# A fused decoder layer whose expert stage packs its tokens into buffers of 96 rows instead of 128, with 18 weight chunks in flight

## What is computed

```python
def hier_moe(x, w_rg, b_rg, w_re, b_re, w_g, w_u, w_d):
    # top-1 of 4 groups, then the top 2 of the 4 experts inside it
    ...
    for e in range(N_EXPERTS):                      # 16
        h = jax.nn.silu(xt @ w_g[e]) * (xt @ w_u[e])   # 1024 -> 512
        out = out + gates[:, e:e + 1] * (h @ w_d[e])   # 512 -> 1024
```

## Time and profile before

| | |
|---|---|
| median of 3 runs | 971.64 us |
| lowest of 3 runs | 970.34 us |
| profiled execution | 972.64 us |
| span of its trace | 970.7 us |
| granted TensorE clock, mean | 0.964 of full |
| busy: PE, DVE, ACT | 907.7 (94%), 669.6 (69%), 491.5 (51%) us |
| weight splits, DVE L1726 | 96 of 2286 ns |
| loads of expert weights | 96 of 1 MB |

### The profile page before, as it was taken

One profiled execution on the slowest core, in us unless ns is written; L12 is line 12 of the kernel. 1 busy time (PEld: TensorE's weight loads), 2 busy tenths in 40 slices (PEclk: granted clock), 3 DMA queues, 4 the chain that ended last, 5 costly groups with the idle time before them and its releaser, 6 DMA issues.

```text
span 970.7 us, 14670 instructions
## 1 busy us (share of the span) xinstructions
PE 907.7 (94%) x5924; PEld 518.1 (53%) x5924; DVE 669.6 (69%) x877; ACT 491.5 (51%) x681; POOL 71.3 (7%) x89
## 2 busy tenths in 40 slices
PE   6999999999999998999999979928999999999884
PEld 4434784855766655444444449924455554545442
DVE  5677769541887775643344344557899999999887
ACT  5444373223454444233232324463787888888643
POOL 7000000003000000000000000010111211111000
PEclk9989999999999999999999989957999999999998
DMA  8702404527621102943443316255899999999742
GB/s 211 176 25 59 116 24 111 151 66 198 176 79 33 38 23 65 391 111 94 120 118 83 104 46 234 95 201 170 295 388 403 380 405 391 389 399 379 309 185 89
DMA packets 119454, 177.92 MB, mean 183 GB/s; under 512 B 14317, under 2 KB 99621, under 8 KB 107094
## 3 DMA queue, kind: packets, MB, share of 16 engines
q1 hardware_dynamic: 112176, 162.76, 48.8%
q0 software_dynamic: 6928, 13.61, 4.8%
q10 hardware_dynamic: 278, 0.56, 0.2%
HBM read 172.76 MB, written 16.22 MB: 195 GB/s over the span
## 4 chain that ended last, share of the span: by engine, by line
PE 88%; DVE 6%; ACT 3%; DMA 1%; issue 1%; DVEq 0%; ACTq 0%; POOLq 0%
PE bank L963 25%; PE bank L964 24%; PE bank L965 24%; PE bank L1176 3%; PE bank L1195 3%; PE bank L1306 2%; DVE arena L1726 1%; PE bank L1070 1%; PE bank L1185 1%; PE bank L1055 1%; ACT arena L839 1%; PE bank L1267 1%; PE bank L1314 1%; PE bank L1134 1%; DMA cst<-in_c_sq 1%
## 5 line engine op out<-in xcount | busy, mean ns | idle before, releaser
L963 PE MATMUL bank<-arena 128*128 128x512 f16 (+1 forms) x1568 | 466.6, 318 | 16.4 <-DVE arena L1832 6.0
L964 PE MATMUL bank<-arena 128*128 128x512 f16 (+1 forms) x1568 | 466.3, 318 | 0.0
L965 PE MATMUL bank<-arena 128*128 128x512 f16 (+1 forms) x1568 | 465.4, 317 | 0.0
L1726 DVE SCALAR_TENSOR_TENSOR arena<-arena 128x2048 f16<-128x2048 f32 x96 | 217.1, 2286 | 42.6 <-ACT arena L839 42.6
L963 PEld LDWEIGHTS bank<-arena 128*128 128x128 f16 x1568 | 155.7, 99 | 146.2 <-issue 36.5
L965 PEld LDWEIGHTS bank<-arena 128*128 128x128 f16 x1568 | 155.1, 99 | 112.6 <-issue 5.4
L964 PEld LDWEIGHTS bank<-arena 128*128 128x128 f16 x1568 | 154.9, 99 | 101.0 <-issue 4.9
L839 ACT ACTIVATE arena<-arena 128x2048 f16<-128x2048 f32 x96 | 181.5, 1908 | 24.8 <-PE bank L965 24.8
L606 ACT ACTIVATE arena<-arena 128x1024 f16<-128x1024 f32 (+1 forms) x92 | 92.5, 1007 | 101.9 <-PE bank L965 76.3
L1471 DVE SCALAR_TENSOR_TENSOR arena<-arena 128x1024 f16<-128x1024 f32 (+1 forms) x91 | 103.5, 1163 | 11.4 <-ACT arena L606 9.9
L660 ACT ACTIVATE arena<-bank 128x512 f32<-128x512 f32 x35 | 20.8, 595 | 92.3 <-PE bank L965 92.2
(11 more groups left out here) (275 smaller groups left out, 766.9 us busy)
## 6 DMA issues: line engine op xcount, KB each, us to landing
arena<-in_moe_wg SPq DMA_DIRECT2D x32, 1024.0 KB, 10.3
arena<-in_moe_wu SPq DMA_DIRECT2D x32, 1024.0 KB, 10.8
arena<-in_moe_wd SPq DMA_DIRECT2D x32, 1024.0 KB, 12.1
arena<-in_w_gate SPq DMA_DIRECT2D x32, 512.0 KB, 4.0
arena<-in_w_in SPq DMA_DIRECT2D x31, 512.0 KB, 3.9
arena<-in_w_branch SPq DMA_DIRECT2D x32, 192.0 KB, 3.6
y_rows<-in_c_tab SPq DMA_DIRECT2D x4, 1024.0 KB, 12.3
arena<-in_w_out SPq DMA_DIRECT2D x8, 512.0 KB, 5.0
```

What stands on the lines that cost most here:

```text
L963: pe.matmul(outb, lhs[0], rhs[0], start=first, stop=False, skip_group_check=True)
L964: pe.matmul(outb, lhs[0], rhs[1], start=False, stop=False, skip_group_check=True)
L965: return pe.matmul(outb, lhs[1], rhs[0], start=False, stop=last_, skip_group_check=True)
L1726: tell("split_done", stt(w_lo[c % NW], stage[c % NS], WSCALE, w_hi[c % NW], ALU.mult, ALU.subtract))
```

## The change

It touches the expert stage and the places of its buffers.

- CAP is 96: packed buffers, one-hots, gathers, scatters and transposes have 96 slots.
- Gate and up are turned round: the stationary operand is a 128 x 128 block of the weights, taken as every second column of a 256-column piece; the moving operand is the 96 packed tokens. A chunk has 48 matmuls of 96 columns instead of 12 of 512. The result has the hidden units on the partitions (`hid`, 4 x 96 = 384 columns), so that the four h transposes go away. Down keeps 12 matmuls of 512 columns per chunk, now with 96 tokens as stationary columns.
- The operations between them work on 384 columns instead of 512; `xg`, `xgT`, `sgr` and `hid` have one buffer instead of two.
- 12 staging buffers instead of 8 (`SLOT` maps chunks to them), 6 split pairs instead of 7 (18 chunks instead of 15), LOOK = 4 instead of 6. 15 loads are issued before the routing branch instead of 13, and the 16th needs no split.
- The scatter of expert e follows the gather of expert e+3 in POOL's queue instead of that of e+4. The four `add_rows` are done at the last four steps. The final norm's gains are loaded later.

```diff
-CAP = P
+CAP = 96
-LOOK = 6
+LOOK = 4
...
-        STAGE = [17408, 24576, 29696, 44172, 46220, 26624, 33292, 35340]
-        EARLY = 5
-        SPLIT = [40076, 42124, 37388, 0, 2048, 6144, 4096]
+        STAGE = [17408, 24576, 29696, 44172, 46220, 26624, 33292, 35340, 4096, 6144, 10752, 15360]
+        SPLIT = [(40076, 41100), (42124, 43148), (37388, 38412), (0, 1024), (2048, 3072), (28672, 31744)]
+        EARLY, READY = 5, 10
+        SLOT = [*range(READY), *range(FIRST), READY, FIRST, READY + 1]
+        for _c in range(len(SLOT), len(STEPS)):
+            SLOT.append(SLOT[_c - NS])
+        def splits_ahead(c):
+            return max((i + 1 for i in range(c) if SLOT[i] == SLOT[c]), default=0)
...
-                src = d["moe_w" + kind][0, e][k * P * hf:k * P * (hf + 1), :].rearrange("(p k) n -> p (k n)", k=k)
-                sp_.dma_start(stage[c % NS], src).then_inc(S(f"stage_landed{c % NS}"), 16)
+                src = d["moe_w" + kind][0, e][k * P * hf:k * P * (hf + 1), :]
+                src = src.rearrange("(p k) n -> p k n", k=k)
+                sp_.dma_start(stage[c].rearrange("p (k n) -> p k n", k=k), src).then_inc(S(f"stage_landed{SLOT[c]}"), 16)
...
-            for c in range(NS, NS + FIRST):
-                sp_.wait_ge(S("split_done"), c - NS + 1)
+            for c in range(READY, READY + FIRST):
+                sp_.wait_ge(S("split_done"), splits_ahead(c))
                 stage_load(c)
+                if c == READY + FIRST - 2:
+                    sp_.wait_ge(S("out_full"), KD)
+                    for j in (READY - 2, READY - 1):
+                        stage_load(j)
...
-                for c in range(NS + FIRST, len(STEPS)):
-                    sp_.wait_ge(S("split_done"), c - NS + 1)
+                for c in range(READY + FIRST, len(STEPS)):
+                    if splits_ahead(c):
+                        sp_.wait_ge(S("split_done"), splits_ahead(c))
+                    elif c > READY + FIRST:
+                        sp_.wait_ge(S("x2_stored"), 16 * NT)
+                        sp_.wait_ge(S("token_full"), 2)
                     stage_load(c)
...
-                            pool.wait_ge(S("xgT_full"), 2 * (e - 1))
+                            pool.wait_ge(S("xgT_full"), 2 * e)
...
-                    if n >= 4:
-                        e = n - 4
+                    if n >= 3:
+                        e = n - 3
...
-                        act.activation(sgr[e % 2], ps[2 * (e % 2)][:, :], ACT.Tanh, scale=0.5 / WSCALE).then_inc(S("sgr_ready"), 1)
+                        act.activation(sgr, ps[2 * (e % 2)][:, 0:KH * CAP], ACT.Tanh, scale=0.5 / WSCALE).then_inc(S("sg_ready"), 1)
...
-                def h_transposes(e):
-                    pe.wait_ge(S("h_ready"), e + 1)
-                    pe.wait_ge(S("xlo_done"), 2 * min(e + 2, NE))
-                    for k in range(KH):
-                        last = pe.transpose(ps[6][:, k * P:(k + 1) * P], hrow[e % 2][:, 2 * P * (k // 2) + k % 2:2 * P * (k // 2 + 1):2], ident)
-                    last.then_inc(S("hgT_full"), 1)
...
                         for k in range(4):
-                            last = products(bank[:, :], (hi[:, 4 * hf + k, :], lo[:, 4 * hf + k, :]),
-                                            (v[0][:, k, :], v[1][:, k, :]), hf == 0 and k == 0, hf == 1 and k == 3)
+                            for m in range(KH):
+                                last = products(bank[:, m * CAP:(m + 1) * CAP], [w[:, k, 2 * P * (m // 2) + m % 2:2 * P * (m // 2 + 1):2] for w in v],
+                                                (hi[:, 4 * hf + k, :], lo[:, 4 * hf + k, :]),
+                                                hf == 0 and k == 0 and m == 0, hf == 1 and k == 3)
...
-                    tell("hlo_done", tt(hgT[e % 2][1].rearrange("p a b -> p (a b)"), ps[6][:, :],
-                                       hgT[e % 2][0].rearrange("p a b -> p (a b)"), ALU.subtract))
+                    tell("hlo_done", tt(hgT[e % 2][1], hid, hgT[e % 2][0], ALU.subtract))
...
-                    if (kind, e, hf) in H_AT:
-                        h_lo(H_AT[kind, e, hf])
+                    if STEPS[c - 1][0] == "u" and STEPS[c - 1][2]:
+                        h_lo(STEPS[c - 1][1])
...
-                        link(stt(sgr[e % 2], sgr[e % 2], 1.0, ps[b0][:, :], ALU.add, ALU.mult))
-                        tell("h_ready", stt(hrow[e % 2], sgr[e % 2], 0.5 * HSCALE / WSCALE ** 2, ps[b0 + 1][:, :], ALU.mult, ALU.mult))
+                        link(stt(sgr, sgr, 1.0, ps[b0][:, 0:KH * CAP], ALU.add, ALU.mult))
+                        tell("h_ready", stt(hid, sgr, 0.5 * HSCALE / WSCALE ** 2, ps[b0 + 1][:, 0:KH * CAP],
+                                            ALU.mult, ALU.mult))
+                    if c >= len(STEPS) - NT:
+                        add_rows(c - len(STEPS) + NT)
```

## The result

The changed kernel takes 964.92 us (median of 20 runs) beside 970.87 us for the kernel before (20 runs). The ratio is 0.9943, 95% interval 0.9933 to 0.9953: a gain of 0.6% where 2.5% had been forecast. The profiled execution has a span of 964.6 us; before it was 970.7.

A forecast was written before the change was run, and what follows sets the result against it. PE bounds the kernel at 17.07 us per expert; after the change DVE would, at 16.1. Start 691.3 + 12 x 16.1 + tail 46.0 + end 15.8 = 946.3 us, plus 0.9, rounded to 947 us; range 938 to 963.

The forecast's parts named there:

- the new PE period: Expert stage: PE needs 14.4 us per expert instead of 17.07, with 96-column matmuls at 42.4 ns each.
- rival A: Gate and up: weight loads set PE's pace; at 61 ns each the whole takes 976 us; chance 0.13.
- DVE's period: Expert stage: DVE needs 15.88 us per expert, plus 0.2 us of waits for ACT: 16.1 us per period.
- The start: Start of the expert stage: x_lo of expert 2 ends at 691.3 us instead of 697.65, 6.3 us sooner.
- The list matmuls (3.9 us): Start of the expert stage: the matmuls for the token lists take 3.9 us on PE, ending at 671.2 us.
- 388 GB/s was the rate beside gathers, but by demand: Expert-stage transfers: the earlier 388 GB/s was taken as what was asked for; 419 GB/s was used for the new period.
- over 72 chunks the lead shrinks by less than 2 us of 32: Expert-stage loads: 2.70 us per chunk at 419 GB/s against DVE's 2.68, so the loads' head start over splits hardly shrinks.
- rival C: Expert stage: transfers set the pace, below about 380 GB/s; with rows cut to 2 or 4 KB, 1022 us; chance 0.06.
- the 962 us: Whole time, about, by a skill page's bound of about 358 GB/s per core from HBM to SBUF.
- Deeper loading is thus worth nothing by itself: Expert-stage loads: the deeper loading only keeps transfers off the path; no gain of its own.
- The tail: From x_lo(14) done to the first add_last: 46.0 us instead of 52.4, DVE's 45.2 plus 0.8 of waits, PE fitting under it.
- rival B: Expert stage: engines hold each other up and PE's clock falls; period stays near 17.07 us, whole 959 us; chance 0.20.

The follow-up runs named there:

- The probe: Changed kernel plus 24 matmuls of 5 moving columns for each of six weight forms (96 or 128 columns, steps 1, 2, 16); ran once, its time not read.
- e3_lead8: Changed kernel, but each load also waits for the split eight chunks back, as if there were 8 staging buffers instead of 12: 975.45 us, ratio 1.0042.
- e8_no_gathers: Changed kernel with gathers that move at most one row, scatters moving all their rows: 955.01 us, ratio 0.9834.

## Why the prediction was wrong

**What bounds the kernel, and the new PE period: right.** Starts of gate and up matmuls were forecast 42.4 ns apart. They are 0.38 us for nine steps, 42 ns. After, timeline of PE:

```profile
705.81 0.21 PE L979 MATMUL bank<-arena 128*128 128x96 f16 x1
...
706.19 0.21 PE L979 MATMUL bank<-arena 128*128 128x96 f16 x1
```

Their weight loads of 128 columns by every second one disappear beneath them, and rival A falls. The fixed part and the price per column, taken from the 128- and 512-column rows, carried down to 96. The probe explains why the nearest row of A misled: L1293 was slow for its step of 16, not for being strided.

**DVE's period: right.** 16.04 us against 16.1, with the five shortened operations at 549 ns in place of 680, and waits for ACT near nothing (2.3 us in 140). The slack of PE didn't cost clock up to 890 us, as priced: the granted clock stays at 1.00, although PE waits nine times for up to 2.8 us, where 2.04 us of waiting had stood before half a clock at 681.94. Behind the longest wait, 3.0 us before 895.66, it did fall: 0.72 on average from 894 to 900 us.

**The start: the term of the list matmuls was mis-sized.** "The list matmuls (3.9 us)" carried over L1293's row, 64 matmuls with 128 weight columns. The diff reduces them to 96 by way of `CAP`, and I took a narrower load to be no dearer. It took 11.64 us, 7.7 more. The rest of the start came 2.7 us better than forecast, in an execution whose clock rose late; by `e3_lead8` it would be 5.1. (The terms that the prediction names for the start add up to 691.1, not 691.3.)

**Transfers: the step that failed is "388 GB/s was the rate beside gathers, but by demand".** My own numbers spoke against it: 6.81 MB in a period of 17.07 us is a demand of 399 GB/s, and the earlier trace rows had 388. Demand was above the rate, so 388 was the ceiling with gathers in the mix, and the landing times of before grew from 8.7 to 15.1 us. I priced the mix at 419 GB/s, taken from a stretch with loads alone, and not quite of the same form (551 of its 1083 packets are under 8 KB), and concluded "over 72 chunks the lead shrinks by less than 2 us of 32". At 388 a chunk with its share takes 2.92 us against DVE's 2.68: 72 times 0.24 is 17 us of lead, and a load needs its own landing time besides. This was rival C's mechanism, with the threshold of 380 GB/s put too low and its chance (0.06) tied to smaller packets, which didn't come: the loads' packets stayed 8 KB. Of the tail's miss, 1.8 to 3.1 us belong here as well: against 52.9 us it is 51.1 without gathers and 49.8 without scatters. That the 962 us given under rival C lie near the measured time is chance: they rest on a slower rate than the 386 to 393 GB/s that were moved. "Deeper loading is thus worth nothing by itself" is true in form, but the four extra buffers are what saves the change: without them it is 0.4% slower than before.

**The tail: rival B's mechanism, in the one place where it applies.** The forecast added DVE's work and 0.8 us of waits. 3.1 us are shown to be ACT's order (tanh and table ahead of splits 94 and 95). The prediction also said that "PE fits under it" and priced a fall of the clock at nothing; here PE was on the chain, and its half clock is worth an estimated 1.9 us. These parts and the transfers' add up to between 6.8 and 8.1 us of a miss of 6.9, so they overlap; only the order and the rows were taken away by a run.

The three misses add up to 18.0 of the 18.3 us. Apart from some 2 us of clock in the first and in the tail, each is a term that was copied from a row which the edit had changed (the lists), taken from a stretch without the disturbance (the rate), or summed for one engine without asking whom it waits for (the tail).

## What to carry to other kernels

When a size shrinks, look up every instruction that the constant reaches: here 64 small matmuls off the main loop took back most of the gain of the start by having fewer weight columns, and putting 128 back gave it to the whole. To learn whether a rate is demand or ceiling, divide a period's bytes by its length and look whether the landing time of like loads grows along the stage; if it does, a shorter period will be paid from the buffers' lead, and the number of buffers decides how long. In a tail, follow each engine's order for an operation that waits ahead of one that others need, and look at the clock behind a long wait of PE.

## What the runs showed of the hardware that was not expected

- A weight load with 5 moving columns behind it: 25 ns for 128 columns at step 1 or 2, 60 at step 16; 44, 46 and 173 for 96 columns. Inside the kernel the 96-column lists at step 16 ran 180 ns apart, at a granted clock of 1.00 and of 0.50 alike: what sets this pace doesn't follow the clock.
- The clock fell while PE was busy with just these matmuls; it had been busy since 657.3 us, without a gap. After, windows in the list matmuls, twice:

```profile
664.20:665.00 0.80, 0.80 (x8) 0.80 (x6) 0.00 (x0) 0.67 (x2) 0.00 (x0) 1.00 0.00 0
668.00:670.00 2.00, 2.00 (x13) 2.00 (x12) 0.00 (x0) 0.42 (x1) 0.00 (x0) 0.50 0.00 0
```

  The clock goes from 2.4 to 1.2 GHz between the two.
- An indirect gather of some 63 rows of 4 KB beside a full queue of loads lowers the total from about 410 GB/s to between 304 and 329 for about 4 us, at full DMA share. Scatters of as many rows leave no such dip: in `e8_no_gathers` no stretch of 2 us from 840 to 890 us is under 365 GB/s.
